# Experts' low parts reordered, `deviation` behind the base's gather, routing's end and the first loads moved

## The chip, the cores and the metric

The kernel runs on one core of a Trainium2 chip. The metric is device time in microseconds, median of three runs. PE is TensorE (PEld its weight loads), DVE is VectorE, ACT is ScalarE, POOL is GpSimd, SP is SyncE, which here only issues transfers.

## The reference, cut to what matters

One layer of a streaming encoder over 4096 frames of 1024 values, all in float32:

```
h   = LN0(concat(meta, x))
mix = (sigmoid(ga) * attention(h) @ w_attn_out + sigmoid(gc) * conv(h) @ w_conv_out) @ w_o
h1  = LN1(alpha * h + mix)
group = argmax(h1 @ w_rg + b_rg)                    # 1 of 4
e1, e2 = top 2 of the 8 experts of that group       # 32 experts in all
y   = sum over e1, e2 of weight_e * (silu(h1 @ w_gate[e]) * (h1 @ w_up[e])) @ w_down[e]
out = LN2(alpha * h1 + y)[without the 16 meta rows]
```

## The kernel before

Each float32 product is made of three passes: weights and rows are split into a high part (`ACT.Copy` into float32r, on ACT) and a low part (raw minus high, on DVE), and PE adds hi x hi, hi x lo and lo x hi (`product`).

**Set-up and mixer.** A first block normalises the 16 meta rows and the first 512 rows and runs ten strips of `w_in` for the meta rows (`meta_strips`, buffers `meta_raw`). The main block then runs over 8 blocks of 512 rows, each 50 strips of weights; `raw` (3 buffers) takes a strip in the first block, where it is split, stored and later loaded again from `split_weights`. During the last eight strips of a block (`wo`), PE transposes the next block's 512 rows (already normalised, in `xs`) into `hT_hi`, `hT_lo`: 8 groups of four 128x128 transposes, at the strips named in `HX_AT`, each followed by a copy of ACT and a subtraction of DVE.

**Route.** After the mixer `route` runs once: DVE chooses group and experts for the last 512 rows, PE counts the ranks, DVE places every row in a list of tiles of 128 rows (each expert has whole tiles), makes the masks `hot_hi` and `hot_lo`, ACT scales them (`listed`), PE multiplies them into `lists`, and DVE reads out `row_index` (which row sits in which slot). `weigh` gives the weights of the two experts from ACT's exponentials. Meanwhile SP loads the 12 chunks of expert 0's weights (each 128x1024, 512 KB: 4 of the gate matrix, 4 of the up matrix, 4 of the down matrix), and ACT splits the first eight (`early`) at the end. The next block cannot begin before every engine has ended this one.

**Experts.** `experts` runs over tiles of 128 rows, expert by expert, 83 tiles for 32 experts. `lo` is an expert's first tile, `swap` its last. Per tile g every engine goes through its queue in order:

- PE: gate products, up products (each needs the chunk's low part), the 8 transposes of the rows of tile g+1, the down products of tile g-1, the 4 transposes of `prod`.
- ACT: silu of the gate, at `swap` four high parts of the next expert's gate, two copies `xT_hi`, at `swap` four of the up matrix, the copy `aT_hi`, at `lo` four of the down matrix, then `measure(g - 1)`: sum and sum of squares of `e_both`.
- DVE: at `swap` four low parts of the next expert's gate; `prod`; `xT_lo` (`evacuate`); `normalise(g - 2)` in two steps; at `swap` four low parts of the up matrix; `aT_lo`; `add_base(g - 1)`, which writes `e_both`; at `lo` the four low parts of the down matrix.
- POOL: with `hold`s (a wait and an empty instruction) between them, `gather_rows(g + 2)`, `store_rows(g - 2)`, `store_part(g - 1)`, `deviation(g - 1)` (the standard deviation's inverse, `rstd`), a wait for the stored part, `gather_base(g)`. Each gather and store of 128 rows is an indirect transfer that POOL issues; for `gather_rows` it waits until the rows are there. The base may only be read when the part before is stored, since a row's second expert adds to what its first one stored.
- SP: loads a chunk of the next expert as soon as its low part is made.

Of the kernel before, what the change touches and what calls it, by code (L numbers as in the profile page):

```python
# [176 lines left out]
def mixer(nc, t, x, w_in, w_attn_out, w_conv_out, w_o, h1, tb, records):  # L177
# [84 lines left out]
    with ExitStack() as ctx:  # L262
# [64 lines left out]
        meta_raw = place([weights + 4 * 4 * D], "meta_raw", [P, META_RAW, D])  # L327
# [31 lines left out]

        with ExitStack() as c1, nc.Block() as block:  # L360
# [4 lines left out]
            raw_in = [sem1(f"meta_raw_in{i}") for i in range(META_RAW)]  # L365
# [22 lines left out]
            def _(sp):  # L388
                def load_strip(n):
                    for dst, src in strip_dmas(*meta_strips[n], meta_raw[:, n % META_RAW, :]):  # L390
                        sp.dma_start(dst, src).then_inc(raw_in[n % META_RAW], 16)
# [145 lines left out]
            def _(pe):  # L537
# [7 lines left out]
                for what, n in order:  # L545
# [12 lines left out]
                    pe.wait_ge(raw_in[n % META_RAW], uses[n % META_RAW])  # L558
# [10 lines left out]
        raw_in = [sem(f"raw_in{i}") for i in range(RAW)]  # L569
# [46 lines left out]
        HX_AT = {WO0 - 1 + i: i for i in range(2 * TILES)}  # L616
# [11 lines left out]
        with nc.Block() as block:  # L628
            @block.sync
            def _(sp):  # L630
# [52 lines left out]
                for s in range(ahead):  # L683
                    load_raw(s)
# [52 lines left out]
            def _(a):  # L737
# [37 lines left out]
                def block_of_strips(b, first):  # L775
                    for s, (kind, i) in enumerate(strips):
# [50 lines left out]
                        if s in HX_AT:  # L827
                            q = HX_AT[s]
# [17 lines left out]
            def _(v):  # L846
# [54 lines left out]
                def block_of_strips(b, first):  # L901
# [33 lines left out]
                    for s, (kind, i) in enumerate(strips):  # L935
# [136 lines left out]
                        if s in HX_AT:  # L1072
                            q = HX_AT[s]
# [33 lines left out]
            def _(pe):  # L1107
# [35 lines left out]
                def block_of_strips(b, first):  # L1143
                    pe.wait_ge(hx_lo, b * 2 * TILES + 1)
                    for s, (kind, i) in enumerate(strips):
# [125 lines left out]
                        if s in HX_AT:  # L1271

                            q = HX_AT[s]
# [43 lines left out]
def route(nc, t, tb, records, keep, weights):  # L1317
# [8 lines left out]
    with ExitStack() as ctx:  # L1326
# [3 lines left out]
        def sem(name):  # L1330
# [7 lines left out]
        upto, first, spare = sb("r_upto", [P, E]), sb("r_first", [P, E]), sb("r_spare", [P, E])  # L1338
        tile_row_f, tile_row = sb("r_tile_row_f", [P, 1]), sb("r_tile_row", [P, 1], I32)
# [12 lines left out]
        hi_made, lo_made, worth_made, listed_up = (  # L1352
            sem("r_hi_made"), sem("r_lo_made"), sem("r_worth_made"), sem("r_listed_up"))

        with nc.Block() as block:
# [9 lines left out]
            def _(po):  # L1365
# [11 lines left out]
                po.wait_ge(got_in, 16)  # L1377

            @block.scalar
            def _(a):  # L1380
                a.wait_ge(diff_ready, 1)
                exponentials(a, r).then_inc(exp_ready, 1)
                for j in range(2 * TILES):
# [5 lines left out]
                for c in range(weights["early"]):  # L1389
                    a.wait_ge(weights["raw_in"][c], 16)  # L1390
                    a.activation(weights["w_hi"][:, c, :], weights["raw"][:, c, :], ACT.Copy)\
                     .then_inc(weights["hi_ready"], 1)

            @block.vector
            def _(v):
                steps = [0]

                def link(ins):
# [10 lines left out]
                v.memset(row_index[:, 0:2, 2:4], int(NOWHERE))  # L1409
                v.wait_ge(counted, 1)  # L1410
# [12 lines left out]
                v.tensor_tensor(tile_row[:, :], tile_row_f[:, :], tile_no[:, :], ALU.add).then_inc(tile_rows_ready, 1)  # L1423
                v.tensor_copy(bounds[:, 0, :], first[:, :])
# [5 lines left out]
                link(v.tensor_scalar(first[:, :], first[:, :], float(P), None, ALU.mult))  # L1430
                link(v.tensor_tensor(r["earlier"][:, :, :], r["earlier"][:, :, :],
                                     ranks[:, 0:TILES * E].rearrange("p (t e) -> p t e", e=E), ALU.add))
                link(place_rows(v, link, r, tb, first))
                v.tensor_scalar(in_tile_i[:, :], tb["slot"][:, :], P - 1, None, ALU.bitwise_and)
                link(v.tensor_scalar(tile_of_i[:, :], tb["slot"][:, :], P.bit_length() - 1, None, ALU.arith_shift_right))
                v.tensor_copy(in_tile[:, :], in_tile_i[:, :])
                link(v.tensor_copy(tile_of[:, :], tile_of_i[:, :]))
                v.wait_ge(exp_ready, 1)
                weigh(v, link, r, tb)
                for j in range(2 * TILES):  # L1440
                    v.tensor_scalar(hot_hi[:, j, :], count_up[:, 0:MT], tile_of[:, j:j + 1], None, ALU.is_equal)\
                     .then_inc(hi_made, 1)
                    v.tensor_scalar(hot_lo[:, j, :], count_up[:, :], in_tile[:, j:j + 1], None, ALU.is_equal)\
                     .then_inc(lo_made, 1)
# [5 lines left out]
                v.tensor_tensor(row_index[:, 2:, 0], code[:, :], second[:, :], ALU.subtract)  # L1450
# [27 lines left out]
def experts(nc, t, h1, out, keep, weights, tb):  # L1478
# [11 lines left out]
    with ExitStack() as ctx:  # L1490
# [7 lines left out]
        rows = sb("e_rows", [P, D])  # L1498
# [9 lines left out]
        minus_mean = sb("e_minus_mean", [P, 1])  # L1508
        rstd = sb("e_rstd", [P, 1])
        x_at, y_at, out_at = sb("e_x_at", [P, 1], I32), sb("e_y_at", [P, 2], I32), sb("e_out_at", [P, 1], I32)  # L1510
# [4 lines left out]
        raw_in, hi_ready, lo_ready = weights["raw_in"], weights["hi_ready"], sem("e_lo_ready")  # L1515
# [4 lines left out]
        rows_in, x_at_set = sem("e_rows_in"), sem("e_x_at_set")  # L1520
# [21 lines left out]
        with nc.Block() as block:  # L1542
# [120 lines left out]
            def _(v):  # L1663
# [43 lines left out]
                for c in range(2 * GC):  # L1707
                    split_lo(0, c)
# [145 lines left out]
```

## Time and profile before

| | us |
|---|---|
| median of 3 runs | 4194.5 (4185.06 to 4198.86) |
| the profiled execution | 4199.52 |
| its span | 4197.5 |
| PE busy in it | 4076.5 (97%) |
| DVE busy | 2073.1 (49%) |
| ACT busy | 1439.2 (34%) |
| POOL busy | 744.8 (18%) |

The mixer's main block runs from 55.1 to about 2630, the route to 2661.6, the experts to the end. A busy PE includes the modelled ends of its products. The issue of indirect transfers counts as POOL's work here; the time that a transfer is on its way does not.

### The profile page before, as it was taken

What the parts mean: (1) busy time and instruction counts of PE and PEld (TensorE: products, weight loads), DVE (VectorE), ACT (ScalarE), POOL (GpSimd) and SP (SyncE); (2) the same over time, 40 slices, a digit from 0 to 9 for tenths busy, and PEclk for the clock granted to TensorE, in tenths of its full rate; (3) what the DMA queues carried; (4) which work ended last, traced back from release to release, by engine and by line L of the source; (5) the groups of instructions that cost most, each with busy time, mean ns of one, the idle gap of its engine ahead of it and who ended that gap; (6) DMA issues with size and microseconds to landing.
All of it is one profiled execution on the core that took longest, in us unless ns stands there. A gap on an engine that the chain in (4) does not pass through costs nothing. (4 is left out here: it accounts for less than half of the span.)

```text
span 4197.5 us, 60770 instructions
## 1 busy us (share of the span) xinstructions
PE 4076.5 (97%) x20066; PEld 3395.4 (81%) x20067; DVE 2073.1 (49%) x3202; ACT 1439.2 (34%) x2543; POOL 744.8 (18%) x1020
## 2 busy tenths in 40 slices
PE   8999999999999999999999998699999999999997
PEld 7888888888888888888888887587888888788886
DVE  3554443443443443443443444577656567665664
ACT  2422311311311311311311311366556456555553
POOL 2000010000000001001001001234333333433333
PEclk9999999999999999999999998799999999999998
DMA  8787456456456455456455555676756566665562
GB/s 251 241 306 244 145 202 204 156 198 196 159 199 195 166 200 187 169 197 187 175 197 184 175 197 186 217 254 222 252 187 205 188 219 229 228 211 190 195 218 81
DMA packets 278468, 840.53 MB, mean 200 GB/s; under 512 B 47952, under 2 KB 99408, under 8 KB 226688
## 3 DMA queue, kind: packets, MB, share of 16 engines
q1 hardware_dynamic: 228400, 716.61, 50.2%
q0 software_dynamic: 49936, 121.90, 8.7%
q8 instruction: 114, 1.87, 0.2%
q14 instruction: 18, 0.15, 0.0%
HBM read 717.60 MB, written 178.45 MB: 213 GB/s over the span
## 5 line engine op out<-in xcount | busy, mean ns | idle before, releaser
L1110 PE MATMUL bank<-hT_hi,w_slot 128*128 128x512 f32 x2176 | 862.3, 396 | 8.3 <-DVE w_slot L898 7.2
L1112 PE MATMUL bank<-hT_hi,w_slot 128*128 128x512 f32 x2176 | 848.9, 390 | 0.0
L1111 PE MATMUL bank<-hT_lo,w_slot 128*128 128x512 f32 x2176 | 848.1, 390 | 0.0
L1742 PE MATMUL e_bank<-e_w_hi,e_xT_hi 128*128 128x512 f32 x1312 | 522.7, 398 | 18.2 <-DVE e_xT_lo L1668 15.8
L1744 PE MATMUL e_bank<-e_w_hi,e_xT_lo 128*128 128x512 f32 x1312 | 514.7, 392 | 0.0
L1743 PE MATMUL e_bank<-e_w_lo,e_xT_hi 128*128 128x512 f32 x1312 | 513.9, 392 | 0.0
L1673 DVE TENSOR_TENSOR e_w_lo<-e_raw,e_w_hi 128x1024 fp32r<-128x1024 f32 x384 | 444.1, 1220 | 116.7 <-ACT e_w_hi L1624 116.7
L1110 PEld LDWEIGHTS bank<-hT_hi,w_slot 128*128 128x128 f32 x2176 | 409.0, 188 | 105.8 <-issue 24.6
L1112 PEld LDWEIGHTS bank<-hT_hi,w_slot 128*128 128x128 f32 x2176 | 408.9, 188 | 87.4
L1111 PEld LDWEIGHTS bank<-hT_lo,w_slot 128*128 128x128 f32 x2176 | 409.5, 188 | 81.2
L1624 ACT ACTIVATE e_w_hi<-e_raw 128x1024 fp32r<-128x1024 f32 x376 | 366.2, 1054 | 2.0 <-issue 2.0
L1742 PEld LDWEIGHTS e_bank<-e_w_hi,e_xT_hi 128*128 128x128 f32 x1312 | 248.3, 189 | 71.7 <-issue 22.5
L1744 PEld LDWEIGHTS e_bank<-e_w_hi,e_xT_lo 128*128 128x128 f32 x1312 | 248.1, 189 | 53.6
L1743 PEld LDWEIGHTS e_bank<-e_w_lo,e_xT_hi 128*128 128x128 f32 x1312 | 248.7, 190 | 50.0
L1742 PE MATMUL e_bank<-e_w_hi,e_aT_hi 128*128 128x512 f32 x664 | 266.5, 401 | 2.7 <-DVE e_both L1682 2.7
L52 POOL TENSOR_SCALAR rstd<-moments 128x1 f32<-128x1 f32 (+1 forms) x69 | 24.8, 359 | 1360.7 <-DVE moments L47 1360.7
L1744 PE MATMUL e_bank<-e_w_hi,e_aT_lo 128*128 128x512 f32 x664 | 260.3, 392 | 0.0
L1743 PE MATMUL e_bank<-e_w_lo,e_aT_hi 128*128 128x512 f32 x664 | 259.7, 391 | 0.0
L766 ACT ACTIVATE work<-bank 128x512 f32<-128x512 f32 x128 | 76.5, 598 | 506.9 <-PE bank L1112 506.9
L1110 PE MATMUL bank<-w_slot,mixT_hi 128*128 128x512 f32 x512 | 206.5, 403 | 0.0
L1630 ACT ACTIVATE e_ignored<-e_both 128x1024 bf16<-128x1024 f32 x83 | 87.5, 1054 | 343.8 <-DVE e_both L1682 343.8
L716 POOL COPY h_rows<-x_rows 128x1024 f32<-128x1024 f32 x32 | 33.2, 1042 | 953.9 <-PE bank L1122 941.2
(330 smaller groups left out, 6712.7 us busy)
## 6 DMA issues: line engine op xcount, KB each, us to landing
w_slot<-split_weights SPq DMA_DIRECT2D x353, 1024.0 KB, 4.8
e_raw<-in_w_exp_gate_dram SPq DMA_DIRECT2D x128, 512.0 KB, 6.0
e_raw<-in_w_exp_up_dram SPq DMA_DIRECT2D x128, 512.0 KB, 6.1
e_raw<-in_w_exp_down_dram SPq DMA_DIRECT2D x128, 512.0 KB, 5.4
split_weights<-w_slot SPq DMA_DIRECT2D x50, 1024.0 KB, 5.7
h_rows<-h_rows SPq DMA_DIRECT2D x64, 512.0 KB, 7.7
x_rows<-in_x_dram SPq DMA_DIRECT2D x32, 512.0 KB, 5.5
raw<-in_w_in_dram SPq DMA_DIRECT2D x30, 512.0 KB, 7.2
```

The lines of the kernel that those rows point to most:

```text
L52: po.tensor_scalar(rstd[0:rows, :], moments[0:rows, 1:2], LN_EPS, None, ALU.add).then_inc(ln_rstd, 1)
L716: po.tensor_copy(h[:, i1, :], xs[:, i1, :]).then_inc(h_copied, 1)
L766: a.activation(w[:, 0:TOK], got, ACT.Sigmoid).then_inc(taken_act, 1)
L1110: pe.matmul(out, hi, x_hi, start=first, stop=False)
L1111: pe.matmul(out, hi, x_lo, start=False, stop=False)
L1112: return pe.matmul(out, lo, x_hi, start=False, stop=last)
L1624: a.activation(w_hi[:, c, :], raw[:, c, :], ACT.Copy).then_inc(split_count(e, c, True)[0], 1)
L1630: a.activation(ignored[:, :], both[:, :], ACT.Copy, accum_out=moments[:, 0, :]).then_inc(summed, 1)
L1673: v.tensor_tensor(w_lo[:, c, :], raw[:, c, :], w_hi[:, c, :].bitcast(FP32), ALU.subtract)\
L1742: pe.matmul(out_p, hi, x_hi, start=first, stop=False)
L1743: pe.matmul(out_p, hi, x_lo, start=False, stop=False)
L1744: return pe.matmul(out_p, lo, x_hi, start=False, stop=last)
```

## The change

Six edits, in one:

1. The first three raw strips are loaded by SP at the end of set-up, so `meta_raw` moves to other memory.
2. `HX_AT` names four strips of `wo` with two groups of four transposes each, in place of eight with one.
3. Route: `weigh` runs ahead of the ranks' count, the `bounds` table is written behind the masks, two low parts of expert 0 are made in the route, ACT makes four of its eight splits ahead of `listed`, and the gather of tile 0's rows is issued inside the route.
4. DVE in the experts: the low parts of the up matrix move from an expert's last tile to the next expert's first; those of the gate are cut two and two around `prod`. At the start DVE makes only the gate's before the rows' own low half.
5. ACT calls silu on a 128x1 tile behind `measure(g - 1)`.
6. POOL: `deviation(g - 1)` moves behind `gather_base(g)`.

```diff
-        HX_AT = {WO0 - 1 + i: i for i in range(2 * TILES)}
+        HX_AT = {WO0 + 2 * i: (2 * i, 2 * i + 1) for i in range(TILES)}
...
+                for s in range(RAW):
+                    for dst, src in strip_dmas(*strips[s], raw[:, s, :]):
+                        sp.dma_start(dst, src).then_inc(raw_in[s], 16)
                 sp.wait_ge(consts_in, 16 * (7 + TAPS))
...
-                for s in range(ahead):
-                    load_raw(s)
                 block_of_loads(0, True)
...
# route, POOL
                 po.wait_ge(got_in, 16)
+                po.wait_ge(first_rows, 1)
+                po.tensor_copy(x_at[:, :], row_index[:, 2:3, 0]).then_inc(weights["x_at_set"], 1)
+                hold(po, weights["x_at_set"], 1)
+                po.indirect_dma_start(out=weights["rows"][:, :], ... x_at ...).then_inc(weights["rows_in"], 16)
# route, ACT
                 exponentials(a, r).then_inc(exp_ready, 1)
+                split_hi(range(weights["early"] // 2))
                 for j in range(2 * TILES):
...
+                split_hi(range(weights["early"] // 2, weights["early"]))
# route, DVE
+                v.wait_ge(exp_ready, 1)
+                weigh(v, link, r, tb)
                 v.wait_ge(counted, 1)
                 count_up_to(...)
...
                 for j in range(2 * TILES):
                     hot_hi, hot_lo
+                bounds (five instructions, before ahead of place_rows)
+                for c in range(weights["done_early"]):
+                    w_lo = raw - w_hi
                 v.wait_ge(listed_up, 1)
# experts, POOL
-                gather_rows(0)
+                hold(po, rows_in, 16)
                 gather_base(-1)
...
                     store_part(g - 1)
-                    deviation(g - 1)
                     hold(po, part_out, g * 16 + 16)
                     gather_base(g)
+                    deviation(g - 1)
# experts, ACT
                         measure(g - 1)
+                        a.activation(unused[:, :], minus_half[:, :], ACT.Silu)
# experts, DVE
                 total = count_tiles(v)
+                for c in range(weights["done_early"], GC):
+                    split_lo(0, c)
+                evacuate(0)
                 v.memset(aT_hi[:, :, :].bitcast(FP32), 0.0)
...
-                for c in range(2 * GC):
-                    split_lo(0, c)
-                evacuate(0)
...
                     with v.Fori(lo, hi) as g:
+                        with v.If(g == lo):
+                            for c in range(GC, 2 * GC):
+                                split_lo(e, c)
                         with v.If(g == swap):
-                            for c in range(GC):
+                            for c in range(GC // 2):
                                 split_lo(e + 1, c)
                         prod
                         evacuate(g * 2 + 2)
+                        with v.If(g == swap):
+                            for c in range(GC // 2, GC):
+                                split_lo(e + 1, c)
                         normalise(g - 2)
-                        with v.If(g == swap):
-                            for c in range(GC, 2 * GC):
-                                split_lo(e + 1, c)
```

## Rows read from the trace of the kernel before

**Rows 1.** Busy time by stretch: length, PE, PEld, DVE, ACT, POOL, PE clock, DMA

```profile
2695.60:4150.60 1455.00, 1430.62 (x6724) 1182.36 (x6722) 937.58 (x1016) 838.42 (x1176) 546.16 (x720) 1.00 0.62 211
```

**Rows 2.** PE's waits over the whole run: total us, times, longest

```profile
PE e_bank L1742 <- DVE e_xT_lo L1668: 15.8, 10, 5.5
...
PE e_bank L1787 <- DVE e_prod L1719: 9.2, 7, 2.9
```

**Rows 3.** Timeline of PE, the transposes of `prod` in two tiles: start, length

```profile
3063.18 0.60 PE L1787 MATMUL e_bank<-ident,e_prod 128*128 128x128 f32 x4
...
3080.90 0.60 PE L1787 MATMUL e_bank<-ident,e_prod 128*128 128x128 f32 x4
```

**Rows 4.** The line of those transposes: ns min/median/max, first and last start

```profile
L1787 PE MATMUL e_bank<-ident,e_prod x328: 270/272/329, 2695.3 to 4168.3; 128*128 128x128 f32 x164
```

**Rows 5.** POOL's groups, 2690.2 to 4109.7: busy us, mean ns, idle before, releasers

```profile
L1572 POOL DMA_INDIRECT h_rows<-e_both,e_y_at x78 | 84.0, 1077 | 37.8 <-issue 19.3 <-DVE e_both L1682 17.9 <-ACT e_ignored L1634 0.6
...
L1582 POOL TENSOR_TENSOR e_rstd<-e_rstd,minus_half 128x1 f32<-128x1 f32 x78 | 54.0, 692 | 11.6 <-POOL e_rstd L1579 0.2
L1586 POOL COPY e_out_at<-row_index 128x1 int32 x78 | 38.8, 497 | 391.4 <-DMA e_rows<-h_rows,e_x_at 391.4
L1563 POOL COPY e_y_at<-row_index 128x2 int32 x78 | 38.0, 488 | 212.3 <-DMA h_rows<-e_both,e_y_at 212.3
L1555 POOL COPY e_x_at<-row_index 128x1 int32 x79 | 32.0, 405 | 16.6 <-PE e_bank L1751 16.2
L1579 POOL TENSOR_SCALAR e_rstd<-e_moments 128x1 f32<-128x1 f32 x78 | 20.4, 262 | 24.0 <-ACT e_ignored L1634 19.7
```

**Rows 6.** Timeline of POOL: start, length, idle before

```profile
2690.20 0.18 POOL L1555 COPY e_x_at<-row_index 128x1 int32 x1 [15.18 <-PE e_bank L1751]
...
3376.33 0.57 POOL L1582 TENSOR_TENSOR e_rstd<-e_rstd,minus_half 128x1 f32<-128x1 f32 x1
```

**Rows 7.** Timeline where the main block opens

```profile
55.09 4.18 SPq L636 DMA_DIRECT2D raw<-in_w_in_dram  x4
...
59.20 1.06 ACT L743 ACTIVATE w_slot<-raw 128x1024 fp32r<-128x1024 f32 x1 [4.38 <-DMA raw<-in_w_in_dram]
...
61.62 0.76 PE L1110 MATMUL bank<-hT_hi,w_slot 128*128 128x512 f32 x1 [7.25 <-DVE w_slot L898]
```

**Rows 8.** Timeline of PE, one group of the next rows' transposes

```profile
2592.08 0.60 PE L1279 MATMUL bank<-ident,x_rows 128*128 128x128 f32 x4
```

**Rows 9.** Timeline, route's end and the experts' first tile

```profile
2647.57 0.17 DVE L135 TENSOR_REDUCE lr_gsum<-lr_gexp 128x4 f32<-128x16 f32 x1
...
2649.34 0.27 DVE L1441 TENSOR_SCALAR r_hot_hi<-r_count_up,r_tile_of 128x98 f32<-128x98 f32 x1
...
2649.64 4.38 ACT L1386 ACTIVATE r_listed<-r_hot_hi,worth 128x98 f32<-128x98 f32 x16 [11.55 <-DVE r_hot_hi L1441]
...
2653.93 7.66 ACT L1391 ACTIVATE e_w_hi<-e_raw 128x1024 fp32r<-128x1024 f32 x8
...
2654.77 0.36 DVE L1446 COPY r_fresh<-r_lists 128x196 f32<-128x196 f32 x1 [2.34 <-PE r_lists L1469]
...
2662.67 0.18 POOL L1555 COPY e_x_at<-row_index 128x1 int32<-128x1 int32 x1 [16.93 <-POOLq L1355]
...
2668.05 1.97 PE L1751 MATMUL e_bank<-ident,e_rows 128*128 128x128 f32 x8 [13.09 <-DMA e_rows<-h_rows,e_x_at]
...
2675.52 0.79 PE L1742 MATMUL e_bank<-e_w_hi,e_xT_hi 128*128 128x512 f32 x1 [5.50 <-DVE e_xT_lo L1668]
```

**Rows 10.** Timeline of DVE at an expert's last tile

```profile
3012.36 4.63 DVE L1673 TENSOR_TENSOR e_w_lo<-e_raw,e_w_hi 128x1024 fp32r<-128x1024 f32 x4
```

**Rows 11.** Timeline of ACT at an expert's change: table load and silu

```profile
3023.39 1.28 ACT L1644 ACT_TABLE_LOAD   x1 [1.79 <-issue]
3024.68 0.60 ACT L1644 ACTIVATE e_act<-e_bank 128x512 f32<-128x512 f32 x1
```

**Rows 12.** DVE's waits, 2720 to 4180: total us, times, longest

```profile
DVE e_both L1682 <- DMA e_base<-h_rows,e_y_at: 88.7, 36, 5.6
```

More of the change, by code:

```diff
@@ L326, in mixer @@
         raw = place([weights + 4 * 6 * D], "raw", [P, RAW, D])
-        meta_raw = place([weights + 4 * 4 * D], "meta_raw", [P, META_RAW, D])
+        meta_raw = place([weights], "meta_raw", [P, META_RAW, D])
         at = [weights + 4 * 8 * D]
@@ L357, in mixer @@
         tp = banks[6:8]
+        raw_in = [sem(f"raw_in{i}") for i in range(RAW)]
         with ExitStack() as c1, nc.Block() as block:
@@ L1423, in _ @@
                 v.tensor_tensor(tile_row[:, :], tile_row_f[:, :], tile_no[:, :], ALU.add).then_inc(tile_rows_ready, 1)
+                link(v.tensor_scalar(start[:, :], first[:, :], float(P), None, ALU.mult))
+                link(v.tensor_tensor(r["earlier"][:, :, :], r["earlier"][:, :, :],
+                                     ranks[:, 0:TILES * E].rearrange("p (t e) -> p t e", e=E), ALU.add))
+                link(place_rows(v, link, r, tb, start))
+                v.tensor_scalar(in_tile_i[:, :], tb["slot"][:, :], P - 1, None, ALU.bitwise_and)
+                link(v.tensor_scalar(tile_of_i[:, :], tb["slot"][:, :], P.bit_length() - 1, None, ALU.arith_shift_right))
+                v.tensor_copy(in_tile[:, :], in_tile_i[:, :])
+                link(v.tensor_copy(tile_of[:, :], tile_of_i[:, :]))
+                for j in range(2 * TILES):
+                    v.tensor_scalar(hot_hi[:, j, :], count_up[:, 0:MT], tile_of[:, j:j + 1], None, ALU.is_equal)\
+                     .then_inc(hi_made, 1)
+                    v.tensor_scalar(hot_lo[:, j, :], count_up[:, :], in_tile[:, j:j + 1], None, ALU.is_equal)\
+                     .then_inc(lo_made, 1)
                 v.tensor_copy(bounds[:, 0, :], first[:, :])
@@ L1429, in _ @@
                 v.memset(bounds[:, 2, E - 1:E], MT)
[L1430 to L1444, printed above, removed]
+                for c in range(weights["done_early"]):
+                    v.wait_ge(weights["hi_ready"], c + 1)
+                    v.tensor_tensor(weights["w_lo"][:, c, :], weights["raw"][:, c, :],
+                                    weights["w_hi"][:, c, :].bitcast(FP32), ALU.subtract)\
+                     .then_inc(weights["lo_ready"], 1)
                 v.wait_ge(listed_up, 1)
@@ L1497, in experts @@
         raw, w_hi, w_lo = weights["raw"], weights["w_hi"], weights["w_lo"]
-        rows = sb("e_rows", [P, D])
+        rows, x_at = weights["rows"], weights["x_at"]
         xT_hi, xT_lo = sb("e_xT_hi", [P, KD, P], F32R), sb("e_xT_lo", [P, KD, P], F32R)
@@ L1508, in experts @@
         minus_mean = sb("e_minus_mean", [P, 1])
+        unused = sb("e_unused", [P, 1])
         rstd = sb("e_rstd", [P, 1])
-        x_at, y_at, out_at = sb("e_x_at", [P, 1], I32), sb("e_y_at", [P, 2], I32), sb("e_out_at", [P, 1], I32)
+        y_at, out_at = sb("e_y_at", [P, 2], I32), sb("e_out_at", [P, 1], I32)
         ident, minus_half = tb["ident"], tb["minus_half"]
@@ L1818, in encoder_block @@
                 sb("bounds", [P, 5, E], I32), slot_tiles)
+        x_at = sb("e_x_at", [P, 8], I32)[:, 0:1]
         F = w_exp_gate.shape[3]
         chunks = 3 * F // P
[L1821 removed]
+        weights = dict(chunks=chunks, early=2 * F // P, done_early=2, raw=sb("e_raw", [P, chunks, D]),
                        w_hi=sb("e_w_hi", [P, chunks, D], F32R),
```

49 lines of the change are left out of this document (27 added, 22 removed).

## The prediction

> **What bounds the kernel now.** I read the stages first, then TensorE's waits, then the queue of each engine that releases it. In the stretch of the experts' tiles TensorE (PE) is busy 1430.6 of 1455 us [rows 1], so on the face of it the kernel is bound by its products and an edit can only gain from PE's gaps. These are few: over the whole run PE waits 15.8 us for the low half of the turned rows and 9.2 us for `prod` [rows 2].
>
> A tile costs PE 17.72 us when nothing holds it (the transposes of `prod` start at 3063.18 and at 3080.90) [rows 3]; from 2695.3 to 4168.3 there are 81 tiles [rows 4], 1473.0 us, so 81 x 17.72 = 1435.3 leaves 37.7 us of loss, waits and clock together.
>
> GpSimd (POOL) does one round per tile: gather rows, store finished rows, store the part, `deviation`, wait for the part, gather the base. From 2690.2 to 4109.7 it does 78 rounds, 18.20 us each. What it waits for other engines in them is small [rows 5]: 17.9 us for DVE's `e_both` ahead of the part's store, 1.0 us for PE at `x_at` (16.2, of which 15.18 end at 2690.20, where the stretch begins [rows 6]), and 19.7 us for ACT ahead of `rstd`, which lie under the part's landing. The large idle terms, 391.4 and 212.3 us, are its own transfers on their way: it issues, waits and goes on. So (1419.5 - 17.9 - 1.0) / 78 = 17.96 us of each round are POOL's own chain, more than PE's 17.72. PE looks busy, yet a queue without slack stands beside it. The forecast rests on this.
>
> **The change part by part.**
>
> *First strips loaded in set-up.* SP issues them at 55.09, when the main block opens; ACT's first split starts at 59.20 and PE at 61.62, 2.42 us behind it [rows 7]. In the new order they follow the last strip of the meta rows, and SP then has nothing else to issue until the block ends. ACT can start at about 55.2, PE at 57.6: **-4.0 us**. Bounds: 0 if the loads slow the meta strips, -5.
>
> *Next rows turned eight at once.* PE leaves its products 4 times per block in place of 8; the transposes are the same 32. Four take 0.60 us [rows 8], and only the edges between them and the products can go. All 64 turnings are 38 us; I take **-1**, bounds 0 and -5. The copies of ACT and DVE come in pairs and end, as before, a strip ahead of the next block.
>
> *Routing's end.* `weigh` takes 1.77 us, 2647.57 to 2649.34, behind `place_rows` [rows 9]. It goes into DVE's wait for the ranks, partly hidden; I charge 0.5 for the rest. With the bounds table's five small instructions (0.4) moved behind the masks, these start at 2647.7, and ACT's `listed`, 4.38 us from 2649.64 before, ends at 2652.4 in place of 2654.0. DVE now makes two low parts (2.4 us) between the masks and `fresh`, so `fresh` comes at 2653.8 in place of 2654.77, and the first row numbers 1.3 later at 2655.1. ACT's eight early splits take 7.66 us from 2653.93 and end the block at 2661.6; with four of them in its wait for the masks the rest end at 2656.3. The gather of the first rows is issued from inside the route: `x_at` at 2655.1 against 2662.67. From there to PE's transposes are 5.4 us (2668.05), so these come at 2660.6. Before, DVE had eight low parts to do ahead of the rows' own, and PE began 7.5 us behind its transposes, at 2675.52. Now two are done in the route and two come while the gather lands; ACT's two copies and DVE's two subtractions remain, 3.5 us: PE begins at 2664.1. **-11.4 us**; bounds -7 (the gather lands 4 later, among loads) and -13. The up half's four low parts come behind the cleared tiles, by my estimate about 8.5 us in, when PE ends the gate half: level, no term.
>
> *Low parts in another order.* DVE's four low parts of the up half (4.63 us at 3012.36) [rows 10] stand ahead of `aT_lo` and `e_both` at an expert's last tile; from `e_both` the chain runs on through ACT's two sums and silu to `prod`. They move to the next expert's first tile, behind `e_both`. The gate half's four are cut two and two around `prod`, which so comes 2.4 us earlier. This takes away most of what makes `prod` late, and with it the rows' low half [rows 2]: at most **-37 us** if nothing else were short.
>
> *Silu called early.* A 128x1 call behind the sums is about 0.2 us of ACT per tile. At an expert's change the table's load starts at 3023.39 after 1.79 us of idle, takes 1.28, and the activation follows at 3024.68 [rows 11]. If the load goes with the early call it hides in that idle: up to 32 x 1.28 us off ACT. If silu keeps its load at L1644, the call does nothing; if both load, ACT has 1.5 us more per tile. I take nothing: POOL decides. The Trainium skill (ScalarE: Activation LUTs, What ACT_TABLE_LOAD costs) adds a drain of 1.38 us to each load; by it a second load per tile would cost ACT 82 x 2.66 = 218 us, an estimate, but here the activation starts 0.01 us behind the load, and the row decides.
>
> *`deviation` behind the base's gather.* Before, it ran while the part was landing: 20.4 + 54.0 us of work and 11.6 + 4.3 of steps between, in front of 212.3 us of waiting for that landing [rows 5]. It cost the round nothing. Behind `gather_base` nothing covers it, and next on the queue is the gather of rows. POOL has no slack, so the round grows by its whole length: 0.26 + 0.14 + 0.57 = 0.97 us with the undisturbed power of [rows 6], 1.16 by the means. The base is not asked for earlier in exchange: the whole 212.3 us of idle ahead of `y_at` end with the part's landing, not with `deviation`.
>
> The sum: 78 x 0.97 = +75.7. POOL's waits for others, 18.9, go, since it is late everywhere: +56.8. It may end the stretch 3 us further behind PE than before, and the last rounds, which have slack, give back 2: +52. Its landings are 391.4 + 322 us in the stretch, of which I put two fifths down to the experts' loads; these are a fixed amount, and over a stretch 4% longer meet fewer landings: -10. **+42 us** for the tiles, DVE's gain included. Bounds: +25 (landings 0.2 shorter a round) and +70 (1.16, no such relief).
>
> Total: -4.0 - 1 - 11.4 + 42 = +25.6 us. The profiled execution took 4199.5 us around its span of 4197.5, 5 above the median of 4194.5. Predicted: **4220 us**, 0.6% slower.
>
> **The rivals.**
>
> 1. *POOL's round does not decide (faster).* With `deviation` in the open the round must still fall under PE's 17.72, so its landings must lose 1.2 us a round once DVE and ACT are punctual. Then most of PE's loss goes: 4194.5 - 16.4 - 30 = 4148. For it: landings vary, and DVE's lateness did cost POOL 17.9 us. Against it: as many weights are loaded as before. Chance 0.22. The Trainium skill (DMA: Bandwidth & Descriptors, Anatomy of one DMA) puts 512 KB at 2.0 + 1.2 = 3.2 us from the issue; by that estimate the round would be near 13 us and this rival would hold. The row of `e_out_at`, 391.4 / 78 = 5.0 us after the issue alone, speaks against it.
>
> 2. *The up half's low parts come late (about the same).* They now wait behind `e_both`, and that waits for the base 36 times, 88.7 us [rows 12]. The gate half is about 5.4 us of a tile. With `e_both` 2.5 us later than its earliest 1.5, the first low part is there at 6.6: 1.2 us in some 20 of 32 experts, +25 against -16 and some -15 of what the order gives, if `deviation` finds cover after all: 4189, within 0.3%. Chance 0.16.
>
> 3. *Both silu calls load the table.* 1.5 us on ACT per tile, in the 30 or so tiles where it is on the way to `prod`; a late POOL hides half: +20 on the forecast, 4240. Chance 0.08.
>
> **How the numbers follow.** My forecast holds 0.54, its own range 4205 to 4245. With rival 3, slower has 0.62, the same 0.16, faster 0.22; 0.3% (12.6 us) is about what a measurement of this kernel can tell from no change. The range reaches from 4155, into rival 1, to 4252, over rival 3.
>
> **What would show it.** Right: POOL's rounds near 18.8 us, `deviation` behind L1566's gather, the idle ahead of `y_at` up from 2.7 to about 4 us a round, PE's loss in the tiles at 75 us or more, shown ahead of the up half and of the turned rows. Wrong: rounds at 17.7, POOL waiting for PE ahead of `x_at` in most tiles, PE's loss below 20 us. PE's first strip should start near 57.6 and the experts' first product near 2659; if that stands at 2664 or later, the route term failed. A second table load per tile shows as 160 of them.

## The result

| | before | after |
|---|---|---|
| median of 7 runs, us | 4189.27 | 4223.76 (4217.41 to 4241.85) |
| the profiled execution | 4199.52 | 4241.85 |
| its span | 4197.5 | 4239.9 |
| 81 tiles of the experts, from the rows of `prod`'s transposes | 1473.0 | 1524.2 |

The ratio of the times is 1.0081, 95% interval 1.006 to 1.0102: 0.8% slower, 34 us. The profiled execution of the kernel after is the slowest of its seven, 18 us over their median; that of the kernel before lies 10 us over its own. So a size read from the one profile below is an upper one: it has twelve long tiles, where the same kernel without silu's call, profiled at its median, has nine.

The line of `prod`'s transposes, as [rows 4] (328 of them, four a tile, are 82 tiles and 81 steps from tile to tile; the 83 named ahead of the prediction is one too many):

```profile
L1806 PE MATMUL e_bank<-ident,e_prod x328: 270/273/276, 2681.5 to 4205.7; 128*128 128x128 f32 x164
```

The experts begin 13.8 us earlier and end 37 us later: their loss over 81 x 17.72 us has gone from 37.7 to 88.9 us. PE's waits in the stretch 2695.6 to 4150.6 have one row, as against [rows 2]:

```profile
PE e_bank L1761 <- DVE e_w_lo L1689: 60.5, 30, 6.3
```

It comes once per expert, in its first tile, ahead of the up half's first product, and is for the low part that was moved there. The waits for the turned rows and for `prod` are gone from this stretch, so the reorder did what it does; it put a larger wait in their place. DVE's timeline at a change of experts in a calm place of the run (the tile's products begin at 3020.3):

```profile
3018.41 1.28 DVE L1704 SCALAR_TENSOR_TENSOR e_done<-e_both,e_minus_mean,e_gain 128x1024 f32<-128x1024 f32 x1
3019.96 1.28 DVE L1709 SCALAR_TENSOR_TENSOR e_finished<-e_done,e_rstd,e_shift 128x1024 f32<-128x1024 f32 x1 [0.27 <-DVE e_done L1704]
3021.27 0.69 DVE L1745 TENSOR_TENSOR e_aT_lo<-e_bank,e_aT_hi 128x512 fp32r<-128x512 f32 x1
3021.88 1.40 DVE L1698 SCALAR_TENSOR_TENSOR e_both<-e_bank,slot_weight,e_base 128x512 f32<-128x512 f32 x2
3025.28 4.63 DVE L1689 TENSOR_TENSOR e_w_lo<-e_raw,e_w_hi 128x1024 fp32r<-128x1024 f32 x4 [2.00 <-issue]
```

and PE's there:

```profile
3025.68 0.39 PE L1763 MATMUL e_bank<-e_w_hi,e_xT_lo 128*128 128x512 f32 x1
3026.55 0.50 PE L1761 MATMUL e_bank<-e_w_hi,e_xT_hi 128*128 128x512 f32 x1 [0.49 <-DVE e_w_lo L1689]
```

`e_both` is here at its earliest. Behind it DVE issues nothing for 2.00 us, as it leaves one expert's loop and enters the next one's (it loads the new bounds in `tiles_of`), and only then come the low parts, the first at 5.0 us of the tile. PE is through with the gate half 5.6 us into the tile, starts the up half 0.6 us late, and the tile comes to 18.5 us in place of 17.7, at best.

The gap is not a fixed price. Of the 30 changes of this run that follow an expert of several tiles, 16 have 2.0 to 2.5 us of it; in 12 it is 0.8 to 1.0 us. Eight of these twelve are calm tiles in which `e_both` began at 2.6 to 2.7 us in place of 1.57, and their first low part still starts at 5.0 us, so up to there a later `e_both` costs nothing. What decides the length of the gap stays open.

A change of experts that is not calm, with POOL's and PE's rows (the products began at 2817.3):

```profile
2819.91 1.29 DVE L1709 SCALAR_TENSOR_TENSOR e_finished<-e_done,e_rstd,e_shift 128x1024 f32<-128x1024 f32 x1 [1.99 <-POOL e_rstd L1597]
2821.11 0.69 DVE L1745 TENSOR_TENSOR e_aT_lo<-e_bank,e_aT_hi 128x512 fp32r<-128x512 f32 x1
2823.32 1.41 DVE L1698 SCALAR_TENSOR_TENSOR e_both<-e_bank,slot_weight,e_base 128x512 f32<-128x512 f32 x2 [1.52 <-DMA e_base<-h_rows,e_y_at]
2826.99 4.63 DVE L1689 TENSOR_TENSOR e_w_lo<-e_raw,e_w_hi 128x1024 fp32r<-128x1024 f32 x4 [2.26 <-issue]
```

```profile
2815.80 0.97 POOL L1578 COPY e_y_at<-row_index 128x2 int32 x1 [5.13 <-DMA h_rows<-e_both,e_y_at]
2817.60 1.18 POOL L1581 DMA_INDIRECT e_base<-h_rows,e_y_at  x1 [0.83 <-POOL e_y_at L1578]
2818.86 0.18 POOL L1594 TENSOR_SCALAR e_rstd<-e_moments 128x1 f32<-128x1 f32 x1
2819.19 0.57 POOL L1597 TENSOR_TENSOR e_rstd<-e_rstd,minus_half 128x1 f32<-128x1 f32 x1
```

```profile
2828.28 0.79 PE L1761 MATMUL e_bank<-e_w_hi,e_xT_hi 128*128 128x512 f32 x1 [5.22 <-DVE e_w_lo L1689]
```

POOL waited 5.13 us for the part to land, the base and `rstd` came late, `e_both` with them, and PE stood 5.22 us. Its products then take 0.79 us in place of 0.39. The windows of the calm tile, of this one, and of the 5.7 us behind the wait (length, busy times of PE, PEld, DVE, ACT and POOL, PE's granted clock, DMA share, GB/s):

```profile
3020.30:3038.80 18.50, 18.01 (x87) 14.70 (x86) 12.04 (x13) 6.25 (x11) 6.38 (x9) 1.00 0.72 250
...
2817.30:2843.10 25.80, 20.58 (x88) 16.56 (x86) 13.01 (x14) 6.37 (x12) 10.39 (x14) 0.87 0.64 210
...
2828.30:2834.00 5.70, 5.70 (x14) 4.50 (x15) 3.33 (x3) 1.88 (x2) 1.92 (x1) 0.53 0.82 240
```

The granted clock is 0.53 over the 5.7 us behind the wait, nearly all of it at the lower of its two levels (1.2 GHz), after PE stood for 5.2 us. PE is busy 20.6 us with the work of 17.7: 2.9 us on top of the wait.

Twelve of the 81 tiles took 20.1 to 26.8 us, each of them an expert's first. In eleven of them `e_both` begins 3.9 to 6.8 us into the tile. The twelfth, the longest, follows the one expert that has a single tile: `e_both` is at its earliest there, but DVE makes the four low parts of that expert's down matrix first, and the first low part of the up half starts at 10.8 us.

POOL's groups in 2695.6 to 4150.6, as [rows 5]:

```profile
L1578 POOL COPY e_y_at<-row_index 128x2 int32 x77 | 28.2, 366 | 307.6 <-DMA h_rows<-e_both,e_y_at 307.6
L1594 POOL TENSOR_SCALAR e_rstd<-e_moments 128x1 f32<-128x1 f32 x77 | 23.3, 302 | 5.8
L1601 POOL COPY e_out_at<-row_index 128x1 int32 x77 | 22.4, 291 | 318.6 <-DMA e_rows<-h_rows,e_x_at 273.2 <-DVE e_finished L1709 45.4
L1570 POOL COPY e_x_at<-row_index 128x1 int32 x77 | 18.9, 246 | 54.2 <-PE e_bank L1770 53.8
```

The idle time ahead of `y_at` is 4.0 us a round, and the rounds are 18.8 us, both as predicted. Two other rows were not: POOL waited for PE ahead of `x_at`, 53.8 us in 32 rounds, which an engine that sets the pace doesn't do; and its idle time ahead of `out_at`, most of it for the rows' landing, fell from 5.0 to 4.1 us a round.

### The profile page after: what moved, and what is told of

It is laid out like the page before. It is cut to its first block and busy times, and to the rows that moved or that the text cites. A ratio compares the mean times of both kernels' runs of the same rounds, so it can differ in the third digit from the quotient of the medians.

```text
span 4239.9 us, 60945 instructions
## 1 busy us (share of the span) xinstructions
PE 4088.0 (96%) x20066; PEld 3407.9 (80%) x20067; DVE 2081.0 (49%) x3202; ACT 1448.7 (34%) x2625; POOL 723.4 (17%) x1020
## 5 line engine op out<-in xcount | busy, mean ns | idle before, releaser
L1761 PE MATMUL e_bank<-e_w_hi,e_xT_hi 128*128 128x512 f32 x1312 | 532.9, 406 | 62.8 <-DVE e_w_lo L1689 61.0
L1109 PE MATMUL bank<-w_slot,mixT_hi 128*128 128x512 f32 x512 | 202.3, 395 | 0.0
L1110 PE MATMUL bank<-w_slot,mixT_hi 128*128 128x512 f32 x512 | 199.6, 390 | 0.0
L1111 PE MATMUL bank<-w_slot,mixT_lo 128*128 128x512 f32 x512 | 199.6, 390 | 0.0
```

The costliest lines, as they stand in the source:

```text
L1109: pe.matmul(out, hi, x_hi, start=first, stop=False)
L1110: pe.matmul(out, hi, x_lo, start=False, stop=False)
L1111: return pe.matmul(out, lo, x_hi, start=False, stop=last)
L1761: pe.matmul(out_p, hi, x_hi, start=first, stop=False)
```

## The experiments

The kernel before was timed again beside them, in four groups (medians 4192.8, 4193.7, 4193.6 and 4193.9), and each ratio is against the kernel before of its own group. Theory P is the prediction's: POOL's round has no slack and sets the pace. Theory L is what the trace above suggests: in an expert's first tile PE waits for the up half's low parts, which stand behind `e_both` and the change of loop.

**The first three parts alone**, with the loop of before:

```diff
-                            for c in range(GC // 2):
+                            for c in range(GC):
                                 split_lo(e + 1, c)
...
-                        with v.If(g == swap):
-                            for c in range(GC // 2, GC):
-                                split_lo(e + 1, c)
...
-                        a.activation(unused[:, :], minus_half[:, :], ACT.Silu)
```

`deviation` and the up half's low parts go back too, as in the edits further down (those of expert 0 are then made ahead of the loop).

> Only the edits ahead of the tiles (strips in set-up, turning in pairs, route's end); the experts' loop is that of the kernel before. Theory P (POOL's round has no slack and sets the pace of the tiles) and theory L (in an expert's first tile PE waits for the up half's low parts, which stand behind DVE's change of loop and behind e_both) agree here: about 16 us faster than before, 4173 us, ratio near 0.996. It gives the base for the other edits. If it is slower or level, the loss does not lie in the loop at all.

4185.15 us, ratio 0.9977 (0.9965 to 0.9988): 8 to 10 us faster, not 20. The profiled execution took 4194.81 us, so its tiles' loss, 40 us, is above what the median has.

**`deviation` behind the gather, alone, on the kernel before:**

```diff
-                    deviation(g - 1)
                     hold(po, part_out, g * 16 + 16)
                     gather_base(g)
+                    deviation(g - 1)
```

> The kernel before with deviation moved behind the base's gather and nothing else. Theory P: +45 to +58 us (4235 to 4247), POOL's rounds near 18.8 us. Theory L: deviation matters only where POOL is late already, so 0 to +15 us, and PE shows no wait for a low part of the weights.

4205.95 us, ratio 1.0033 (1.0019 to 1.0046): +13, where the prediction's term, +42 with bounds of +25 and +70, had POOL's round grow by its whole length. What became of it stands in two of POOL's groups of this run:

```profile
L1586 POOL COPY e_out_at<-row_index 128x1 int32 x80 | 57.0, 713 | 323.7 <-DMA e_rows<-h_rows,e_x_at 313.7 <-DVE e_finished L1693 9.9
L1563 POOL COPY e_y_at<-row_index 128x2 int32 x79 | 27.0, 342 | 302.0 <-DMA h_rows<-e_both,e_y_at 302.0
```

The idle ahead of `y_at` grew by 1.1 us a round (2.7 to 3.8), as predicted. The wait for the rows' landing shrank from 5.0 to 4.0 us a round [rows 5]. The rows' gather is issued right behind the base's, which lands 4.0 us after its issue, so the two transfers are on their way together. With `deviation` between them the rows' gather starts 1.20 us later behind the base's issue (2.47 in place of 1.27, means of 79 rounds). Its own issue takes 0.29 us more (1.44 in place of 1.15) and the landing behind that 0.96 us less: counted from its start it lands 0.67 us sooner, over half of the 1.20. The part lands 0.23 us sooner too (3.85 in place of 4.08), and the round comes to 18.36 us in place of 18.16.

**The kernel after with `deviation` put back:**

```diff
+                    deviation(g - 1)
                     hold(po, part_out, g * 16 + 16)
                     gather_base(g)
-                    deviation(g - 1)
```

> The changed kernel with deviation back ahead of the wait for the part. Theory P: the whole loss of the loop goes, 4223 - 50 = 4173 us or less. Theory L: the tiles where rstd comes late are relieved, but the 0.8 us per expert that DVE's change of loop costs stays (31 x 0.8 = 25 us), so about 4190 us, and PE still waits 31 times for w_lo, 25 to 35 us in all.

4212.41 us, ratio 1.0059 (1.0038 to 1.0079): some 10 us of the 34, with tiles' loss still at 57 us and five tiles over 20 us in place of twelve. Both theories missed: P said 4173 or less, L about 4190. The interval overlaps that of the kernel after, 1.006 to 1.0102.

**The kernel after with the up half's low parts put back** into the tile before:

```diff
-                        with v.If(g == lo):
-                            for c in range(GC, 2 * GC):
-                                split_lo(e, c)
...
                         normalise(g - 2)
+                        with v.If(g == swap):
+                            for c in range(GC, 2 * GC):
+                                split_lo(e + 1, c)
```

> The changed kernel with the up half's low parts back in an expert's last tile, deviation still behind the gather. Theory P: no gain, 4220 to 4240 us. Theory L: the waits of PE for w_lo (61 us and the half clock behind the long ones) go, 4165 to 4180 us, unless POOL's lateness comes out elsewhere.

4193.18 us, ratio 1.0004 (0.9995 to 1.0014). `deviation` is in its late place here, and yet the loss is gone. Theory P said 4220 to 4240 and falls. Theory L's 4165 to 4180 missed as well, by 13 us. The edit also makes expert 0's low parts ahead of the loop. PE's waits in the stretch:

```profile
PE e_bank L1763 <- DVE e_w_lo L1689: 11.1, 12, 2.1
PE e_bank L1763 <- DVE e_xT_lo L1684: 10.5, 18, 0.8
```

**The same low parts at the end of the last tile**, ahead of the change of loop, with `deviation` late and early:

```diff
                         add_base(g - 1)
+                        with v.If(g == swap):
+                            for c in range(GC, 2 * GC):
+                                split_lo(e + 1, c)
```

> The kernel after, with the up half's low parts moved from the top of an expert's first tile to the end of the tile before it: behind e_both's two halves as now, but ahead of DVE's change of expert loop (the 2.0 us of issue between e_both and the first low part). Deviation stays behind the gather. Theory L with the loop's change as its main part: the regular first tiles lose their 0.8 us (some 19 of 31, 15 us) and the twelve long ones up to 2 us each, so 4185 to 4210 us, and PE's mean wait for w_lo under 1 us (it was 1.97 us over 31 tiles). Theory L with e_both as its main part (what counts is that the low parts stand behind e_both at all, which waits for rstd and base): only a little of it comes back, 4212 to 4224 us, and PE's wait for w_lo stays above 1.2 us. Theory P (POOL's round sets the pace): 4220 to 4230 us, as PE's time is not what decides.

> As up_tail, and deviation put back ahead of the gather. If deviation's place costs some 8 to 13 us by itself (it was +13.2 alone on the kernel before, and 11.4 less when undone in the kernel after), this one is 8 to 13 us under up_tail. If it costs only where PE or DVE is already late at an expert's change, the difference to up_tail is under 5 us. With the loop's change as the main part of theory L: 4175 to 4198 us. With e_both as the main part: 4200 to 4213 us, as undoing deviation alone gave 4212.

4249.67 us (1.0137, 1.0123 to 1.0152) and 4246.09 us (1.0121, 1.0104 to 1.0137). Every time expected was missed, theory L's by the most; only the 4 us between the two are as one branch had them (under 5, if `deviation` costs something only where PE or DVE is late already). The low parts do follow `e_both` at once, so the gap went with the change of loop; but `e_both` is later: it begins 5.1 us into an expert's first tile in the first of them and 5.3 in the second, where the kernel after has 3.2 (means of 31). DVE in the first of these kernels (the tile's products began at 2771.7):

```profile
2774.92 1.29 DVE L1709 SCALAR_TENSOR_TENSOR e_finished<-e_done,e_rstd,e_shift 128x1024 f32<-128x1024 f32 x1 [2.00 <-POOL e_rstd L1597]
2776.12 0.68 DVE L1744 TENSOR_TENSOR e_aT_lo<-e_bank,e_aT_hi 128x512 fp32r<-128x512 f32 x1
2778.14 1.41 DVE L1698 SCALAR_TENSOR_TENSOR e_both<-e_bank,slot_weight,e_base 128x512 f32<-128x512 f32 x2 [1.33 <-DMA e_base<-h_rows,e_y_at]
2779.46 4.62 DVE L1689 TENSOR_TENSOR e_w_lo<-e_raw,e_w_hi 128x1024 fp32r<-128x1024 f32 x4
```

Its idle time ahead of `y_at` is 379.6 us in 76 rounds, 5.0 each: the part's landing takes longer still. So what counts here is not the 2 us of the loop's change but when `e_both` comes, and behind that POOL's transfers.

**Both back** (the edits of the two runs before these), so that only the divided gate half and silu's call stay of the loop's change:

> The kernel after with both the up half's low parts and deviation back: what is left of the change in the loop is the gate half's low parts two and two, and silu's call. Undoing the up half alone gave 4193.2 us, the first three parts alone gave 4185.2 us; this run divides the 8 us between deviation and the divided gate half. If deviation is all of it: 4183 to 4188 us. If the divided gate half (two low parts now stand behind xT's low parts and ahead of e_both) is a cost of its own: 4190 to 4194 us.

4192.29 us, ratio 0.9997 (0.9988 to 1.0007), within the 4190 to 4194 that the expectation gives a divided gate half with a cost of its own.

**Without silu's call:**

```diff
-                        a.activation(unused[:, :], minus_half[:, :], ACT.Silu)
```

> The kernel after without the one-element silu call behind measure. If the call does nothing (the table is still loaded at the long silu, 82 times, and the call runs 0.19 us on an engine with over 10 us of idle time a tile): 4217 to 4230 us, no difference to the kernel after within its own spread. Rival: the call and its issue time on ACT delay the next copies: 4 to 10 us less than the kernel after, at 0.1 us a tile.

4226.40 us, ratio 1.0084 (1.0069 to 1.0098): no difference (its profile, which is at its median, has a tiles' loss of 75 us, which fits the 34 us of the result better than the 89 above). In the kernel after the table is loaded ahead of the long silu as before, not at the call:

```profile
L1659 ACT ACT_TABLE_LOAD  x82: 1283/1283/1283, 2662.6 to 4193.7; - x82
```

**Half of each weight load.** POOL's timelines of the kernel before show why `e_both` comes at such different times. Two rounds, the part's store and the wait behind it:

```profile
2776.09 0.99 POOL L1572 DMA_INDIRECT h_rows<-e_both,e_y_at  x1 [0.30 <-issue]
...
2782.82 0.18 POOL L1563 COPY e_y_at<-row_index 128x2 int32 x1 [4.75 <-DMA h_rows<-e_both,e_y_at]
...
2832.70 0.99 POOL L1572 DMA_INDIRECT h_rows<-e_both,e_y_at  x1 [0.31 <-issue]
...
2836.43 0.19 POOL L1563 COPY e_y_at<-row_index 128x2 int32 x1 [1.75 <-DMA h_rows<-e_both,e_y_at]
```

From the end of the store's issue to the next copy it is 5.74 us in one and 2.74 in the other. I sorted the rounds by whether ACT splits an expert's down half in their tile, that is, whether the tile is an expert's first; there that expert's raw chunks come free and the next expert's loads run (mean us from the end of the store's issue to `y_at`; rounds of 2690 to 4151):

| | down half split there | other rounds |
|---|---|---|
| before | 6.1 (32) | 2.8 (48) |
| before, half loads | 3.6 (32) | 2.2 (50) |
| after | 4.8 (30) | 3.5 (47) |
| after, half loads | 2.8 (31) | 2.4 (49) |
| low parts at the tail | 6.0 (30) | 4.3 (47) |
| first three parts alone | 6.1 (31) | 2.7 (49) |

Theory T: the loads of the next weights lengthen POOL's landings, and these set how late `e_both` is. Its two runs load half of each chunk in the loop; what is computed with the rest of each chunk is old data, all else is the same.

```diff
-                        load_expert_chunk(sp, t, weights, e + 1, c)
+                        load_half_chunk(sp, t, weights, e + 1, c)
```

> The kernel before, in which each load of an expert's weights in the loop brings only half of its chunk (the output is not the reference's; every instruction of the engines is as before). It is the base for after_half: by how much the weights' loads stretch POOL's round. Theory T (a partial sum's store, S, takes 6.2 us to land in the rounds at an expert's change against 2.8 to 3.1 us in others, because the loads of the next weights run then; that makes these rounds 19.5 to 20.1 us): the landing at the change falls to 3 to 4 us, POOL's x_at waits for PE in most tiles, the 81 tiles lose 5 to 20 us instead of 37, and the time is 4160 to 4180 us. If the loads have no part in it: landings and time as before, within 5 us of 4193 us.

> The kernel after with the same halved loads of the weights (output not the reference's). Theory T: with short landings rstd and base come in time, e_both starts 1.5 us into every tile, and all that the up half's place costs is the regular 0.8 us in each of 31 first tiles; the long first tiles of 20 to 26 us are gone. Tiles' loss 20 to 32 us; time 4160 to 4178 us, at most 12 us over before_half, with the 5 to 8 us of the first three parts in its favour. If the lateness of e_both comes from DVE's and POOL's own order and not from the loads: the long first tiles stay and the time stays over 4205 us, some 30 us over before_half.

4170.24 us (ratio 0.9950, 0.9935 to 0.9965) and 4188.71 us (0.9989, 0.9980 to 0.9998). The transposes of `prod` in them, before and after:

```profile
L1800 PE MATMUL e_bank<-ident,e_prod x328: 270/272/329, 2694.6 to 4139.3; 128*128 128x128 f32 x164
```

```profile
L1819 PE MATMUL e_bank<-ident,e_prod x328: 271/272/273, 2680.2 to 4154.1; 128*128 128x128 f32 x164
```

Tiles' losses are 9.4 and 38.6 us. In the kernel before, three quarters of what PE's tiles lost (28 of 37.7 us) is gone with half of the loads; POOL now waits 75.8 us for PE ahead of `x_at`, and `e_both`, in the tiles that are not an expert's first, begins at 1.7 us in place of 3.6. In the kernel after, all but two of the long first tiles are gone and the regular one stays: 18.4 to 19.0 us in 29 first tiles, 25 us over 17.72 together, of the 29 between the two. The two that stay, 23.6 and 27.6 us, are the one at the first change of experts and the one behind the expert with a single tile. The time, 4188.71, lies over its forecast of 4160 to 4178, and the 18.5 us between the two runs are more than the 12 I allowed; the forecast of 20 to 32 us of loss missed by the two long tiles.

**Route's end alone:** the kernel before with the `route` part of the change, so that of the kernel after this goes (and the loop's edits, as above):

```diff
-                for s in range(RAW):
-                    for dst, src in strip_dmas(*strips[s], raw[:, s, :]):
-                        sp.dma_start(dst, src).then_inc(raw_in[s], 16)
...
-        HX_AT = {WO0 + 2 * i: (2 * i, 2 * i + 1) for i in range(TILES)}
+        HX_AT = {WO0 - 1 + i: (i,) for i in range(2 * TILES)}
```

> The kernel before with the change of the route's end alone (set-up's strips, the turning of the next rows and the loop as before). Its experts should begin with x_at near 2657 us, and the first expert product near 2667 us, some 11 us earlier than before; with nothing else that is 4182 us. But every kernel with the first three parts ended 12.8 us after the start of its last store, 9.6 us of it behind the store's landing with no engine and no queue at work, where the kernel before ended 4.1 us after the start of that store, with 3.5 us of issue ahead of it: 5.3 us longer in all. If that comes with route's longer code, this kernel shows it too: 4186 to 4189 us and a last store issued 0.85 us behind its copy. If it comes with set-up's or the mixer's edit: 4181 to 4184 us and the end as before.

4188.94 us, ratio 0.9996 (0.9987 to 1.0005). The first expert product starts at 2665.6, 9.9 us earlier than [rows 9]; the gain is 4.6 us by the medians and 1.7 by the ratio, whose interval holds no change. The end of the program took most of the rest back. Before, the last store stood 3.50 us behind its copy and the span (4197.5) ended 4.0 us behind the store's start:

```profile
4189.76 0.18 POOL L1586 COPY e_out_at<-row_index 128x1 int32 x1 [1.64 <-DVE e_finished L1693]
4193.44 1.07 POOL L1588 DMA_INDIRECT out_dram<-e_finished,e_out_at  x1 [3.50 <-issue]
```

With route's change alone (span 4191.2):

```profile
4177.31 0.18 POOL L1600 COPY e_out_at<-row_index 128x1 int32 x1 [1.65 <-DVE e_finished L1707]
4178.34 1.08 POOL L1602 DMA_INDIRECT out_dram<-e_finished,e_out_at  x1 [0.85 <-POOL e_out_at L1600]
```

From the copy's end to the span's it is 13.7 us in place of 7.5: 6.2 us more (the 5.3 of the expectation was added up wrongly). In the kernel after the same store has landed 3.2 us behind its start, and in the 9.6 us from there to the end no engine and no queue shows work. All eleven profiles with route's change end 12.8 us behind the start of the last store, the three without it 4.0. So the cost belongs to that part; what happens in it stays open.

**Two weight loads under way at most,** on the first three parts alone, loads whole:

```diff
                         hold(sp, *split_count(e, c, False))
+                        if c >= 2:
+                            hold(sp, raw_in[c - 2], e * 16 + 32)
+                        else:
+                            hold(sp, raw_in[c + CH - 2], e * 16 + 16)
                         load_expert_chunk(sp, t, weights, e + 1, c)
```

> The first three parts alone (loop as before, as front_only, 4185.2 us), and in the loop the load of an expert's chunk is issued only when the chunk two before it has landed, so that at most two loads are under way where the kernel before has about four. All loads bring their whole chunks. Theory T (what POOL's round loses at an expert's change is lost to the burst of weight loads): the partial sum's store there lands in 4 to 5 us instead of 6.2, the 81 tiles lose 15 to 30 us instead of 40, and the time is 4165 to 4178 us, under both kernels. If the number of bytes and not their order decides (the loads take the same share of the queues, only longer), the landings stay near 6 us or other rounds pay for it: 4180 to 4190 us. If two under way are too few where an expert has one tile (some 12 loads in 17.7 us), PE waits for weights there: over 4190 us.

4189.21 us, ratio 0.9993 (0.9984 to 1.0002). The part's landing where the down half is split fell from 6.1 to 4.9 us, and in the other rounds rose from 2.7 to 3.6: the same bytes, spread out, gave to some rounds and took from others. The profile's tiles' loss, 36 us, is no gain on the 40 of the first three parts alone, which was read from an execution 10 us over its median; by the ratios this kernel is 7 us slower than that one, with intervals that just overlap. No version that loads whole weights beats the first three parts alone, which beat both kernels.

## Why the prediction came out as it did

The time was right, 4220 against 4223.8, and so was the sign; of the reasons, half. That the number is so near is luck: the forecast added -16.4 and +42, the runs give -10, +8, +3 and +32, and the largest of them was in a rival.

*The term of +42 for `deviation` behind the gather* is the step that failed. It stood on "POOL has no slack, so the round grows by its whole length". Alone the move costs 13 us, under the lower bound of 25; on the kernel with the first three parts and the divided gate half, it costs 3 (ratios 0.9997 and 1.0004, whose intervals overlap); undone in the kernel after it is worth 9 (intervals that overlap too). The landings were taken as nearly fixed lengths, 10 us of relief in all; two transfers that overlap give back 0.67 of the 1.20 us by which one is put off, and the round grew by 0.20 us, not by 0.97. That rounds of 18.8 us and 4.0 us ahead of `y_at` did show was no proof: POOL's rounds are as long as PE's tiles, whoever sets them.

*Rival 2, the up half's low parts late behind `e_both`*, had the mechanism. Moving them costs 32 us (ratios 1.0004 and 1.0081; 26 with `deviation` in its old place, 0.9997 and 1.0059), the whole of the result but for small terms. I priced it at +25 and set 31 us of gain against it, 16 from the first three parts and 15 from the new order. Of the 16 some 10 came, of the 15 nothing: most of what PE's tiles lost before went with half of the loads (37.7 us, 9.4 with half loads), without any change in the order of the low parts. And I missed DVE's change of loop: the first low part comes at 5.0 us at the earliest, which makes even a punctual first tile 0.8 us long, 25 us in 29 tiles of the run with half loads, and not 1.2 in 20. The rest are the long tiles, where a late base meets a PE that has no other work, and the lower clock behind it.

*Rival 1* was right in what it says of POOL (landings become shorter by 1 us, it waits for PE at `x_at`) and wrong in what it concludes, since the up half took the place of POOL.

*Set-up and turning, -5.* PE's first strip starts at 59.50, not at the 57.6 predicted. ACT was in time at 55.31, but beside POOL's copies DVE's first low part started 1.10 us behind ACT's first split, where before, with the copies done, it was 0.03 (59.20 + 1.06, then 60.29); and the first two took 1.95 us each, where the next, with POOL done, takes 1.21:

```profile
55.31 2.95 ACT L744 ACTIVATE w_slot<-raw 128x1024 fp32r<-128x1024 f32 x3 [0.35 <-PEq L361]
55.33 4.97 POOL L717 COPY h_rows<-x_rows 128x1024 f32<-128x1024 f32 x4 [12.66 <-POOLq L361]
57.47 3.90 DVE L898 TENSOR_TENSOR w_slot<-raw,w_slot 128x1024 fp32r<-128x1024 f32 x2 [7.87 <-ACT w_slot L744]
...
59.50 0.77 PE L1109 MATMUL bank<-hT_hi,w_slot 128*128 128x512 f32 x1 [4.98 <-DVE w_slot L898]
```

So -2.1. Of both parts together single profiles tell little: in the ten kernels that have them, the first expert product starts between 2659.4 and 2662.7 (2662.2 in the kernel after), 2660.6 in the mean, against 2665.6 in the one run with route's change alone. By the mean that is -5.0, as forecast, but how much of it is the turning is not shown.

*Route's end, -11.4.* It measured -9.9 at the first product. From `x_at` to PE's transposes it took 6.7 us, not 5.4 (2651.79 to 2658.46). The rows themselves landed as before, 5.3 us behind `x_at`; but the transposes began 1.3 us behind the landing, at the change from the route's block to the next one, where before they began at once. The 6.2 us at the end of the program had no term. With them the account closes: 14.6 us earlier in the mean at the first product, 6.2 us later at the end, and 8 to 10 us measured.

*Silu's call, 0*, was right: it loads no table and costs nothing. *The reorder of the gate half* had no term of its own; the kernel with it is 8 us slower than the one without (ratios 0.9977 and 0.9997). Their profiles show the same tiles' loss, 40 us, but the first was read from an execution 10 us over its median and the second from one at its median, so the 8 us may well lie in the tiles. In their profiles `e_both` begins 7.5 us into an expert's first tile without the divided gate half and 8.6 with it, and 3.8 and 4.2 in the others; that this is the cost is not shown.

By ratios of a 4190 us kernel: first three parts -10, divided gate half and call +8, `deviation` +3, up half +32; together +34.

What stays open besides: why the low parts at the tail of the last tile are worse than at the top of the first. That POOL's landings are 1 us longer there is shown; that the raw chunks then come free just as the part is stored is only argued.

## What to carry to other kernels

An engine whose time goes into its own transfers has no fixed round: put work between two transfers that overlap, and the second can land sooner by half of it or more, as here. Ask of every piece of work that is moved what it now stands behind, including the engine's change of loop, and what that in turn waits for: here a preparation that stood ahead of its time went behind a chain that hangs on a DMA's landing. And a row that comes out as forecast bears out the mechanism only if the rival would give another.

## What the runs showed of the hardware

- At DVE's change from one inner loop to the next, with three loads of bounds, it issued nothing for 2.0 to 2.5 us in 16 of 30 changes and for 0.8 to 1.0 us in 12.
- In an expert's first tile, POOL's next copy came 6.1 us behind the issue of a store of 512 KB by row indices, and 3.6 us with half of the weights' bytes on the queues (means of 32).
- A two-input DVE instruction of 128x1024 took 1.95 us beside POOL copies of the same size and 1.21 behind them (at 61.50).
- After a wait of 5.2 us PE's granted clock was 0.53 for the next 5.7 us.
- Behind the last landing of the program 0.8 us passed in the kernel before and 9.6 us in the kernel after, with nothing in the trace.
